# Second feed-forward block: squares summed by VectorE, weights issued ahead of the h store, and head 0's q, k, v loaded during the value jobs

## What is computed

```python
for i in range(2):
    hn = rmsnorm(h, e_norm[0] if i == 0 else o_norm[0])
    if i == 0:                       # even half
        qa, fa, ia, za, xb, zb = split(hn @ e_w_in)
        ya = head_rmsnorm(hgrn2(qa, fa, ia)) * silu(za)
        yb = rg_lru(causal_conv(xb)) * silu(zb)
        mix = concat(ya, yb) @ e_w_out
    else:                            # odd half
        qk, v, og, z, ig, fg = split(hn @ o_w_in)
        q, k = split(silu(causal_conv(qk)))
        mix = (head_rmsnorm(mlstm(q, k, v, ig, fg)) * sigmoid(og) * silu(z)) @ o_w_out
    h = h + mix
    h = h + sigmoid(h @ ple_gate_w[i]) * rmsnorm(p[i] @ ple_w[i])
```

## Time and profile before

| | us |
|---|---|
| median of 3 runs (4039.8 to 4046.36) | 4044.81 |
| the profiled execution, its own time | 4041.37 |
| its span in the profile | 4039.6 |
| TensorE matmul busy | 3636.9 (90%) |
| VectorE busy | 2006.1 (50%) |
| ScalarE busy | 1514.1 (37%) |
| GpSimd busy | 454.4 (11%) |

### The profile page before, as it was taken

One profiled execution on the slowest core, in us unless ns is written; L12 is line 12 of the kernel. 1 busy time (PEld: TensorE's weight loads), 2 busy tenths in 40 slices (PEclk: granted clock), 3 DMA queues, 4 the chain that ended last, 5 costly groups with the idle time before them and its releaser, 6 DMA issues. The chain is left out here.

```text
span 4039.6 us, 50439 instructions
## 1 busy us (share of the span) xinstructions
PE 3636.9 (90%) x20182; PEld 2997.2 (74%) x20182; DVE 2006.1 (50%) x3086; ACT 1514.1 (37%) x2512; POOL 454.4 (11%) x349
## 2 busy tenths in 40 slices
PE   6699999899647679889999979999999799989998
PEld 2288888787546558778888768787899688867786
DVE  6555555364566533644555553435533344444454
ACT  1322222244445343445655642324222344432332
POOL 1000000042221000211100140020000000013011
PEclk8899999899878789899999989999999899999999
DMA  9343343223232253142322153335755657634332
GB/s 353 122 159 129 102 133 108 88 55 103 95 99 85 68 161 97 49 144 87 94 86 81 61 161 97 91 95 94 120 121 98 111 100 106 112 82 118 94 91 87
DMA packets 585418, 437.93 MB, mean 108 GB/s; under 512 B 63734, under 2 KB 519874, under 8 KB 583904
## 3 DMA queue, kind: packets, MB, share of 16 engines
q1 hardware_dynamic: 578272, 414.88, 39.3%
q10 hardware_dynamic: 6048, 19.14, 1.2%
q0 software_dynamic: 864, 0.67, 0.1%
HBM read 381.31 MB, written 53.26 MB: 108 GB/s over the span
## 5 line engine op out<-in xcount | busy, mean ns | idle before, releaser
L1910 DVE TENSOR_TENSOR w_lo<-w,w_hi 128x512 fp32r<-128x512 f32 x446 | 305.3, 699 | 623.8 <-ACT w_hi L1903 623.5
L1903 ACT ACTIVATE w_hi<-w 128x512 fp32r<-128x512 f32 x446 | 273.6, 627 | 594.0 <-PE od_acc L1889 185.2
L3663 PE MATMUL ta_acc<-ta_x_hi,w_hi 128*128 128x512 f32 x1024 | 403.6, 394 | 13.1 <-DVE ta_x_lo L3803 8.2
L3773 DVE TENSOR_TENSOR w_lo<-w,w_hi 128x512 fp32r<-128x512 f32 x260 | 208.8, 806 | 404.3 <-ACT w_hi L3691 402.8
L3665 PE MATMUL ta_acc<-ta_x_hi,w_lo 128*128 128x512 f32 x1024 | 400.8, 391 | 0.0
L3664 PE MATMUL ta_acc<-ta_x_lo,w_hi 128*128 128x512 f32 x1024 | 400.5, 391 | 0.0
L3691 ACT ACTIVATE w_hi<-w 128x512 fp32r<-128x512 f32 x260 | 164.0, 631 | 505.4 <-PE ta_acc L3665 474.0
L1887 PE MATMUL ev_acc<-ev_u_hi,w_hi 128*128 128x512 f32 x680 | 283.1, 416 | 43.2 <-DVE ev_u_lo L2636 18.4
L1887 PE MATMUL od_acc<-od_u_hi,w_hi 128*128 128x512 f32 x768 | 305.4, 398 | 1.3 <-DVE od_u_lo L2533 0.9
L1888 PE MATMUL od_acc<-od_u_lo,w_hi 128*128 128x512 f32 x768 | 299.8, 390 | 0.0
L1889 PE MATMUL od_acc<-od_u_hi,w_lo 128*128 128x512 f32 x768 | 299.8, 390 | 0.0
(11 more groups left out here) (631 smaller groups left out, 8188.8 us busy)
## 6 DMA issues: line engine op xcount, KB each, us to landing
w<-in_o_w_in_dram SPq DMA_DIRECT2D x260, 256.0 KB, 8.1
p_w<-in_w_in_dram SPq DMA_DIRECT2D x72, 512.0 KB, 5.0
w<-in_e_w_in_dram SPq DMA_DIRECT2D x144, 256.0 KB, 2.9
mod_w<-in_w_ada_dram SPq DMA_DIRECT2D x8, 4096.0 KB, 23.4
w<-in_ple_gate_w_dram SPq DMA_DIRECT2D x128, 256.0 KB, 2.8
gate_w<-in_w_ada_dram SPq DMA_DIRECT2D x16, 1024.0 KB, 6.0
z_w<-in_w_in_dram SPq DMA_DIRECT2D x64, 256.0 KB, 2.9
w<-in_e_w_out_dram SPq DMA_DIRECT2D x64, 256.0 KB, 2.9
```

Of the source, the lines that this page charges most:

```text
L1903: act.activation(self.w_hi[m % self.ring][:], self.w[m % self.ring][:], ACT.Copy).then_inc(self.hi_set, 1)
L1910: eng.tensor_tensor(self.w_lo[m % self.ring][:], self.w[m % self.ring][:], self.w_hi[m % self.ring][:].bitcast(F32), ALU.subtract).then_in ...
L3663: pe.matmul(bank, hi, hi_x[:, k, :], start=(k == 0), stop=False)
L3773: dve.tensor_tensor(w_lo[m % RING][:], w[m % RING][:], w_hi[m % RING][:].bitcast(F32), ALU.subtract).then_inc(lo_set, 1)
```

## The change

In `MixedInput`, ScalarE writes the square of block k into `mixed[k]` (no longer needed once h has it) and needs no wait; VectorE, not GpSimd, adds the squares, after its last `low`, with the low parts of chunks 80 to 83 in the middle and of 84 to 87 at the end; ScalarE makes the high parts up to chunk 87 before it waits for the sum. SP issues the weights to chunk 87 before it waits for h; `wr` and `wi` wait for the last add. TensorE does 12 steps of f1 before the sum's matmul and 4 behind it. In `odd_stage`, SP loads head 0's k, q, v after the work of job number 20, with waits for the stores of jobs 0, 9 and 17, into tiles of their own that do not lie on the early ones; the wait for the tables on SP is gone.

```diff
@@ Projection @@
+    def wait_job_stored(self, eng, n):
+        eng.wait_ge(self.stored[n % 2], 16 * (self.store_no[n] + 1))
@@ MixedInput.act @@
             if k == 0:
                 act.wait_ge(self.mix_sums, 1)
-            if k >= 5:
-                act.wait_ge(self.added, k - 4)
-            act.activation(self.total if k == 0 else self.y_ring[k % 4], self.h[:, k, :], ACT.Square).then_inc(self.sq_set, 1)
+            act.activation(self.total if k == 0 else self.mixed[k], self.h[:, k, :], ACT.Square).then_inc(self.sq_set, 1)
+        proj.split_high(act, self.base + 3 * proj.ring)
         act.wait_ge(self.sums_ready, 1)
-        act.wait_ge(self.u_set, KD)
@@ MixedInput.dve @@
         low(KD - 1)
+        for k in range(1, KD):
+            if k == KD // 2:
+                proj.split_low(dve, self.base + 2 * proj.ring + 4)
+            dve.wait_ge(self.sq_set, k + 1)
+            if k > 1:
+                dve.wait_ge(self.added, k - 1)
+            dve.tensor_tensor(self.total, self.total, self.mixed[k], ALU.add).then_inc(self.added, 1)
+        proj.split_low(dve, self.base + 3 * proj.ring)
         dve.wait_ge(self.inv_set, 1)
-
-    def pool(self, pool):
-        for k in range(1, KD):
-            pool.wait_ge(self.sq_set, k + 1)
-            if k > 1:
-                pool.wait_ge(self.added, k - 1)
-            pool.tensor_tensor(self.total, self.total, self.y_ring[k % 4], ALU.add).then_inc(self.added, 1)
@@ even_stage, sync @@
             proj.sp_upto(sp, KD * plan.LEAD)
+            proj.load_weights(sp, norm.base + 3 * proj.ring)
             sp.wait_ge(norm.h_set, KD)
             sp.dma_start(h_dram.rearrange("b p t -> p b t"), h[:]).then_inc(h_kept, 16)
+            sp.wait_ge(norm.added, KD - 1)
             sp.dma_start(wr[:], a["b_w_r_2"].rearrange("l n c d -> c (l n) d")).then_inc(w_lru_in, 16)
@@ even_stage, tensor @@
             proj.pe_upto(pe, KD * (plan.LEAD + 3))
+            proj.pe_steps(pe, KD - 4)
             norm.pe_sums(pe)
-            proj.pe_steps(pe, KD // 2)
+            proj.pe_steps(pe, 4)
             pe.wait_ge(norm.inv_set, 1)
@@ even_stage, gpsimd @@
-            norm.pool(pool)
-
@@ odd_stage @@
+    FIRST_LOAD, FIRST_MADE = 20, (0, 9, 17)
...
+        q_in, k_in = ([sb(f"{n}_in0", LAT)] for n in "qk")
+        v_tok = [sb("v_tok0", ML_CH, ML_E * P)]
...
-        q_in, k_in = ([sb(f"{n}_in{b}", LAT, owner=late) for b in range(2)] for n in "qk")
-        v_tok = [sb(f"v_tok{b}", ML_CH, ML_E * P, owner=late) for b in range(2)]
+        q_in, k_in = ([tiles[0], sb(f"{n}_in1", LAT, owner=late)] for n, tiles in (("q", q_in), ("k", k_in)))
+        v_tok = [v_tok[0], sb("v_tok1", ML_CH, ML_E * P, owner=late)]
@@ odd_stage, sync @@
             for n in range(EARLY):
                 proj.sp_upto(sp, KD * (n + 1))
+                if n == FIRST_LOAD:
+                    for made in FIRST_MADE:
+                        proj.wait_job_stored(sp, made)
+                    load(0)
...
             proj.wait_stored(sp)
-            sp.wait_ge(tabs_set, 1)
...
-            load(0)
             for hd in range(ML_H):
```

More of the change, by code:

```diff
@@ L3261, in _, with load @@
             sp.dma_start(p_tok[:], a["p_2"][1, 0].rearrange("(m p) f -> p m f", p=P)).then_inc(p_in, 16)
+            def load(hd):
+                b = hd % 2
+                sp.dma_start(k_in[b][:], qk_dram[hd + ML_H]).then_inc(loaded[b], 16)
+                sp.dma_start(q_in[b][:], qk_dram[hd]).then_inc(loaded[b], 16)
+                sp.dma_start(v_tok[b][:], v_view[:, :, ML_E * P * hd:ML_E * P * (hd + 1)]).then_inc(loaded[b], 16)
             for n in range(EARLY):
                 proj.sp_upto(sp, KD * (n + 1))
+                if n == FIRST_LOAD:
+                    for made in FIRST_MADE:
+                        proj.wait_job_stored(sp, made)
+                    load(0)
                 if n == GATE_JOB:
@@ L3268, in _ @@
             proj.wait_stored(sp)
-            sp.wait_ge(tabs_set, 1)
-            def load(hd):
-                b = hd % 2
-                sp.dma_start(k_in[b][:], qk_dram[hd + ML_H]).then_inc(loaded[b], 16)
-                sp.dma_start(q_in[b][:], qk_dram[hd]).then_inc(loaded[b], 16)
-                sp.dma_start(v_tok[b][:], v_view[:, :, ML_E * P * hd:ML_E * P * (hd + 1)]).then_inc(loaded[b], 16)
-            load(0)
             for hd in range(ML_H):
```

## The result

Five runs of each kernel on the same chip: 4018.72 us in the median after the change (4012.83 to 4021.99), 4042.92 before (4038.09 to 4046.36). The ratio is 0.9938, with a 95% interval from 0.9928 to 0.9949: faster by 24 us. The forecast was 4021.6 in a range of 4010 to 4031.

The account below looks back on a forecast made before the run. TensorE, busy 90% of the span, was taken as the bound, so gains come from its idle or low-clock stretches: -12.9 (even half) and -10.3 (odd half) make -23.2, forecast 4021.6 us, range 4010 to 4031.

Parts of the forecast that it names:

- VectorE's loop without GpSimd: Even half: with GpSimd's 15 adds gone a VectorE step takes 1.99 us, and TensorE starts block 3 3.1 us earlier.
- Adds on VectorE: Even half: 15 dependent adds at 0.73 us, 11 us in VectorE's tail, end at 1718.9; TensorE wants the sum at 1727.7.
- Weights ahead of the store: Even half: chunks 80 to 87 issued early, the 7.33 us stall goes, f1 is through at 1731.9 against 1748.9.
- SP's wait for the adds: Even half: SP's new wait delays small weights and later loads, yet chunk 91 is in by about 1729, wanted at 1736.
- What is late next: Even half: the evacuation chain puts the first attention product at 1739.8, TensorE standing 8 us there instead of 3.67.
- Even half: Opening of the second feed-forward's even half, up to the first attention product: -12.9 us, bounds -9 and -15.
- Odd half: Start of head 0: TensorE no longer waits for q, k, v but for a weight split; -10.3 us, bounds -7.8 and -20.5.
- The sum: Both halves: -23.2 us, the profiled execution from 4041.37 to 4018.2, and 4021.6 as the forecast median.
- the one with a quick last store: Odd half, rival: the last value store lands fast, TensorE never stands in head 0, 10.2 us more gone, 4011.4; chance 0.12.
- The rival in which SP's new wait hurts: Even half: small loads issue as slowly as now, chunks 88 to 91 in at 1740, 4 us back, 4025.6; chance 0.07.
- the slower one: Even half, rival: VectorE's adds end so late that SP's wait decides, from 1749 on; 8.1 us slower, 4052.9; chance 0.02.
- The weighing of the 512 B rule: Odd half: line rate from 512 B would make the sum -33.4; the prediction kept the trace's 17.4 us store instead.

Follow-up runs that it names:

- adds_on_gpsimd: The changed kernel with the 15 adds of squares back on GpSimd, reading the tiles they read now, the weights still ahead of the store: 4031.18 us.
- more_adds: The changed kernel with each of the 15 adds of squares on VectorE followed by one more add of the same size into a scratch tile: 4023.99 us.
- gates_from_q_columns: The changed kernel with head 0's four gate jobs reading their weights from the columns of queries 0 to 3 (wrong gates, for timing only): 4009.73 us.
- wide_rows: The changed kernel with head 0's gate chunks 132 to 147 read as 2 rows of 256 columns, not 4 of 128 (wrong gates, for timing only): 4003.26 us.
- no_store_wait: The changed kernel without ScalarE's and VectorE's waits for the value stores ahead of head 0, SP's own moved to before head 1's load: 4012.06 us.
- store_on_scalare: The changed kernel with the store of the last value job (job 24) issued by ScalarE in place of SP: 4021.91 us.

## Why the prediction was right

Its mechanism and its sizes held, step by step; times of the changed kernel are set on the old axis by the loops' starts (1663.67 and 1665.07).

- VectorE's loop without GpSimd: block 3 was to start 3.1 us earlier; it did by 3.13 (9.43 from the loop's start against 12.56). adds_on_gpsimd brings the old loop back to 0.02 us.
- Adds on VectorE: end forecast at 1718.9, came at 1719.6 (in the chain they start 0.79 us apart and not 0.73); sum wanted at 1727.7, came at 1727.85. more_adds shows the slack.
- Weights ahead of the store: f1 and the turns through at 1731.9, came at 1732.0. The 2.03 and 7.33 us stalls and the slow matmuls behind them are gone.
- SP's wait for the adds: chunk 91 in by 1729, came at 1729.05, and was split 7 us later.
- What is late next: a stall of 8 us, then 7.89; the product at 1739.8, then 1739.9. Even half -12.9 forecast, -12.8 measured.
- Odd half: -10.3 forecast, -9.9 measured. That it is so close is in part luck. The store landed 17.5 us after the broadcasts where it had been 16.6, which costs 0.9; the half job behind the stand took 7.1 us and not 7.7, which gives 0.6 back (the restart lost 1.6 us to the low clock and not 2.2). The turns and products of q and k take 1.25 us (3138.79 to 3140.04) and not 2.5, which only makes the stand longer, as the end is the store's. So the stand was 10.26 us and not 8. The stretch behind it, from the add products to the stage's last matmul, is 416.37 us in both kernels, so the gain did carry to the end.
- The sum: 23.2 forecast, 24.2 measured in the medians, 21.7 in the two profiled spans. The forecast time of 4021.6 is 2.9 over the measured one, 1.9 of it because the kernel before had a median of 4044.81 in the three runs then known and 4042.92 in five. That a sum of two places comes within 1 us of a difference of medians is luck too, as the untouched stages alone move by several us.

Of the rivals, the one with a quick last store was the nearest miss in kind. It did not happen (18.2 us, after 17.4 before the change), but gates_from_q_columns, wide_rows and no_store_wait show that its 10.2 us were really there to be had: 10.4 to 12.0. The rival in which SP's new wait hurts found the small loads issued in 0.37 us; the slower one wanted adds that end past 1749.

Two readings outside the sum need a word. The earlier trace rows is not the store just before the last: that one took 17.6 us in the same trace, so the rival of a fast last store had less for it than its chance of 0.12 took from that row. And the prediction left open how the loads ahead hold the store; my later reading, that it stands in line on SyncE's queue, was wrong, as from ScalarE's queue it took as long (store_on_scalare). The weighing of the 512 B rule came out for the rows: "DMA: Bandwidth & Descriptors" of the Trainium skill puts line rate from 512 B up (Specifications), here pieces of 512 B ran at 41 GB/s with the DMA engines 74% busy, and pieces of 1024 B in the same place took the delay away. The prediction was right to keep the slow store in its sum.

## What to carry to other kernels

When a store or load is slow, look at the piece length of what runs beside it before moving it to another queue: as many bytes in 1024 B pieces landed in 4.4 us where 512 B pieces took 19.0. A wait that guards a buffer is worth checking against what is really written next; here, where only head 1's q, k and v lie on the stored tiles, one guarded nothing on two engines and cost 10 us. An order that two engines share is worth moving on both: here a step forward on one came back as a wait two levels later.

## What was not expected of the hardware

- A GpSimd add of 128x512 beside VectorE costs VectorE 1.0 us for each add, whether it falls on a product or on a scaled subtraction: 1.76 against 0.69 and 0.74 us.
- Strided loads of 512 B pieces from one matrix ran at 41 to 44 GB/s for stretches of 10 us and more, with the DMA engines anywhere from 52 to 95% busy, and in another stretch, from other columns, at 138 (62% busy).
- Adds in a chain on VectorE start 0.79 us apart, and unrelated ones can be put between them at 0.60 each without much delay to the chain: 15 extra adds cost 5.7 us and not 15 times 0.69.
